# Reordering the seven-product scheme of a SwiGLU up-projection, with twice the accumulating banks

## The reference

```python
def _swiglu(x, w13, w2):
    h = x @ w13                       # (512 x 1024) @ (1024 x 5632), D_FF = 2816
    g, u = jnp.split(h, 2, axis=-1)
    return (jax.nn.silu(g) * u) @ w2
...
x = _layer_norm(ALPHA * x + _swiglu(x, ffn_w13[i], ffn_w2[i]), ln2_g[i], ln2_b[i])
```

## Time and profile before

| | |
|---|---|
| time, median of 3 runs | 2188.87 us (2188.75 to 2191.24) |
| the profiled execution | 2189.42 us, its span 2187.2 us |
| PE busy | 2153.1 us (98% of the span), 13192 matmuls |
| DVE busy | 1515.6 us (69%) |
| ACT busy | 887.5 us (41%) |
| POOL busy | 538.5 us (25%) |
| PE clock granted | full in all 40 slices |
| DMA | 204.33 MB, mean 93 GB/s |

### The profile page before, as it was taken

The page is one execution under the profiler, slowest core; times in us unless marked ns, Lnnn a source line. Parts: engine busy times, 40 slices in busy tenths (PEclk is TensorE's granted clock), DMA queues, the critical chain, the costliest instruction groups (busy, mean ns, idle before and its releaser), DMA issues.

```text
span 2187.2 us, 34709 instructions
## 1 busy us (share of the span) xinstructions
PE 2153.1 (98%) x13192; PEld 1891.8 (86%) x13192; DVE 1515.6 (69%) x2037; ACT 887.5 (41%) x1554; POOL 538.5 (25%) x370
## 2 busy tenths in 40 slices
PE   9999999999999999999999999999999999999998
PEld 7777899998888988999888899988887778999887
DVE  3787688963479977898534789943538867889434
ACT  3455444442233423444322444432325554444322
POOL 0000255620030003565200356500000003565000
PEclk9999999999999999999999999999999999999999
DMA  6211323333333022334431333342232113333421
GB/s 212 68 58 48 104 80 109 105 116 106 106 96 97 1 76 78 88 107 115 156 96 53 102 87 97 101 131 96 77 116 68 52 61 100 87 97 99 133 96 58
DMA packets 256744, 204.33 MB, mean 93 GB/s; under 512 B 6256, under 2 KB 235760, under 8 KB 256608
## 3 DMA queue, kind: packets, MB, share of 16 engines
q1 hardware_dynamic: 252976, 189.42, 29.0%
q0 software_dynamic: 3632, 13.02, 1.9%
HBM read 200.32 MB, written 2.10 MB: 93 GB/s over the span
## 4 chain that ended last, share of the span: by engine, by line
PE 91%; DVE 5%; issue 2%; ACT 1%; DMA 1%; SPq 0%; POOL 0%; DVEq 0%; POOLq 0%; ACTq 0%
PE ps L1485 18%; PE ps L1487 18%; PE ps L1486 18%; PE ps L1564 10%; PE ps L1565 9%; PE ps L1566 9%; DVE hid L1263 3%; PE ps L1779 2%; PE ps L1802 1%; PE ps L1610 1%; PE ps L1791 1%; PE ps L1782 1%; PE ps L1930 0%; PE ps L2025 0%; DVE x_nat L1026 0%
## 5 line engine op out<-in xcount | busy, mean ns | idle before, releaser
L967 DVE TENSOR_TENSOR w_lo<-raw,w_hi 128x1024 fp32r<-128x1024 f32 x212 | 278.5, 1322 | 343.2 <-ACT w_hi L586 342.4
L586 ACT ACTIVATE w_hi<-raw 128x1024 fp32r<-128x1024 f32 x212 | 220.5, 1055 | 423.9 <-PE ps L1487 372.0
L1395 DVE TENSOR_TENSOR w_lo<-raw,w_hi 128x512 fp32r<-128x512 f32 (+1 forms) x256 | 297.0, 1170 | 43.9 <-ACT w_hi L652 43.7
L1485 PE MATMUL ps<-w_hi,a_hi 128*128 128x512 f32 x832 | 325.9, 392 | 0.3 <-DVE w_lo L967 0.2
L1487 PE MATMUL ps<-w_hi,a_lo 128*128 128x512 f32 x832 | 323.9, 389 | 0.0
L1486 PE MATMUL ps<-w_lo,a_hi 128*128 128x512 f32 x832 | 323.8, 389 | 0.0
L1564 PE MATMUL ps<-t_hi,w_hi 128*128 128x256 f32 x1024 | 293.5, 287 | 4.9 <-DVE over_lo L1404 0.9
L1485 PE MATMUL ps<-xT_hi,w_hi 128*128 128x512 f32 (+1 forms) x760 | 292.6, 385 | 4.9 <-issue 3.7
L1565 PE MATMUL ps<-t_lo,w_hi 128*128 128x256 f32 x1024 | 289.6, 283 | 0.0
L1566 PE MATMUL ps<-t_hi,w_lo 128*128 128x256 f32 x1024 | 289.5, 283 | 0.0
L1487 PE MATMUL ps<-xT_hi,w_lo 128*128 128x512 f32 (+1 forms) x760 | 285.6, 376 | 0.0
(11 more groups left out here) (170 smaller groups left out, 4151.2 us busy)
## 6 DMA issues: line engine op xcount, KB each, us to landing
raw<-in_w SPq DMA_DIRECT2D x264, 512.0 KB, 4.0
raw<-in_wqkv SPq DMA_DIRECT2D x48, 512.0 KB, 3.9
raw<-in_pw SPq DMA_DIRECT2D x24, 512.0 KB, 4.1
raw<-in_wo SPq DMA_DIRECT2D x16, 512.0 KB, 3.7
ln_gb<-in_g POOLq DMA_DIRECT2D x8, 512.0 KB, 4.5
ln_gb<-in_b POOLq DMA_DIRECT2D x8, 512.0 KB, 5.8
x_nat<-in_x SPq DMA_DIRECT2D x4, 512.0 KB, 6.1
out<-x_nat SPq DMA_DIRECT2D x3, 512.0 KB, 2.6
```

What stands on the lines that cost most here:

```text
L586: nc.scalar.activation(weight_hi(u), raw[:, r, :], ACT.Copy).then_inc(w_hi_done, 1)
L967: nc.vector.tensor_tensor(weight_lo(u), raw[:, r, :], weight_hi(u).bitcast(f32), ALU.subtract).then_inc(w_lo_done, 1)
L1395: nc.vector.tensor_tensor(to, src, hi.bitcast(f32), ALU.subtract).then_inc(form_lo[g], 1)
L1485: nc.tensor.matmul(dst, lhs[0], rhs[0], start=start, stop=False, skip_group_check=check)
```

## The change

All of it lies in the seven-product stage and at its end; the products, their matmuls and the forms stay the same in number and size.

- PE's order in block p becomes A11(p), A22(p-1), S2(p), A12(p), S4(p-1), S3(p), S1(p).
- The banks: A11 and A12 use one of the banks of the whole units; S2, S3 and A22 alternate between two banks by the block's parity, and so do S1 and S4. S2 and S1 wait for the reader of two blocks before.
- S4's form has two places, by parity.
- The kept sums lie in buffers that attention uses (`mix_gb`, `o_nat`) instead of the weight ring's free quarter; u2 has two places.
- DVE's order: c22(p-1), low S4(p), low S1(p), c21(p-1), low A22(p), u2(p), gating(p-2), c12(p-1), low A1(p+1), u3(p), low S23(p+1). ACT's: high S4(p), S1(p), copy of A11(p), high A22(p), `first_tokens(p)`, high A1(p+1), `last_tokens(p-1)`, high S23(p+1).
- The loads of a block also wait for the low part of A22, now the last form made.
- At the end of the stage the splits of chunks 20 and 21 and the last sums have another order, the gating of block 14 among them; before a pooling layer POOL's loads into `mix_gb` wait for the gating of block 15.

```diff
@@ -132,9 +132,9 @@
     order = []
     for p in range(SEVENS):
         if p == 0:
-            order += [(p, f) for f in ("A11", "S2", "A12", "S1", "S3")]
+            order += [(p, f) for f in ("A11", "S2", "A12", "S3", "S1")]
         else:
-            order += [(p, "A11"), (p - 1, "A22"), (p - 1, "S4"), (p, "A12"), (p, "S2"), (p, "S1"), (p, "S3")]
+            order += [(p, "A11"), (p - 1, "A22"), (p, "S2"), (p, "A12"), (p - 1, "S4"), (p, "S3"), (p, "S1")]
     return order + [(SEVENS - 1, "A22"), (SEVENS - 1, "S4")]
 
 
@@ -142,7 +142,7 @@
 FORMS = len(FORM_NUMBER)
 G_A1, G_S1, G_S23, G_A22, G_S4 = range(5)
 FORM_GROUP = {"A11": G_A1, "A12": G_A1, "S1": G_S1, "S2": G_S23, "S3": G_S23, "A22": G_A22, "S4": G_S4}
-FORM_PLACE = {"A11": (0, 0), "A12": (0, 1), "S2": (1, 0), "S3": (1, 1), "A22": (2, 0), "S4": (2, 1), "S1": (3, 0)}
+FORM_PLACE = {"A11": (0, 0), "A12": (0, 1), "S2": (1, 0), "S3": (1, 1), "A22": (2, 0), "S1": (3, 0)}
 T3, T1, T2, T4 = range(4)
 
 
@@ -210,11 +210,8 @@
     xT_lo = sb("xT_lo", [P, KD, SEQ], f32r)
     hid = sb("hid", [P, FC * SEQ])
     raw = sb("raw", [P, RING, UNIT])
-    shared3 = -(-nc.sbuf_base // 32) * 32
     w_hi = sb("w_hi", [P, RING, UNIT], f32r)
     w_lo = sb("w_lo", [P, RING, UNIT], f32r)
-    over_hi = nc.alloc_sbuf_tensor_at("over_hi", [P, RING, UNIT], f32, offset=shared3)
-    over_lo = nc.alloc_sbuf_tensor_at("over_lo", [P, RING, UNIT], f32, offset=shared3 + RING * UNIT * 4)
     shared1 = -(-nc.sbuf_base // 32) * 32
     a_hi = sb("a_hi", [P, RING, SEQ], f32r)
     a_lo = sb("a_lo", [P, RING, SEQ], f32r)
@@ -361,18 +358,19 @@
 
         return ring_number(unit0[i, "up"] + 2 * SEVEN_TO + q) % RING
 
-    def form(tiles, i, f):
-
-        q, h = FORM_PLACE[f]
+    def form(tiles, i, p, f):
+
+        q, h = (2 + p % 2, 1) if f == "S4" else FORM_PLACE[f]
         return tiles[:, seven_slot(i, q), h * BANK:(h + 1) * BANK]
 
-    def sums_kept(i):
-
-        return [w[:, seven_slot(i, 3), BANK:2 * BANK].rearrange("p (h n) -> p h n", h=2) for w in (over_hi, over_lo)]
-
-    def seven_bank(i):
-
-        return (up_bank(i, "up") + 4) % 8
+    firsts = mix_gb[:, 0, 0:SEQ].rearrange("p (h n) -> p h n", h=2)
+    u2 = tuple(o_nat[:, 2 * h:2 * h + 2, :].rearrange("p t n -> p (t n)") for h in range(2))
+    u3 = mix_gb[:, 0, SEQ + HALF:2 * SEQ]
+
+    def seven_bank(i, p, f):
+
+        other = (up_bank(i, "up") + 4) % 8
+        return {"A11": up_bank(i, "up") + 1, "A12": up_bank(i, "up") + 1, "S1": other + 2 + p % 2, "S4": other + 2 + p % 2}.get(f, other + p % 2)
 
     def used(i, p, f):
@@ -437,6 +435,7 @@
                     if SEVEN_FROM <= c - 2 < SEVEN_TO:
                         p = SEVENS * i + c - 2 - SEVEN_FROM
                         sp.wait_ge(form_lo[G_S4], p + 1)
+                        sp.wait_ge(form_lo[G_A22], p + 1)
                         sp.wait_ge(form_lo[G_S1], p + 1)
                         sp.dma_start(raw[:, u % RING, :].rearrange("p (k n) -> p k n", n=P), src).then_inc(raw_loaded[u % RING], 16)
                     else:
@@ -533,6 +532,7 @@
                         nc.gpsimd.tensor_tensor(top[:, BANK:2 * BANK], top[:, BANK:2 * BANK], s23[:, 0, :], ALU.subtract).then_inc(form_sum, 1)
                 if to_pooling(n + 1):
                     j = (i + 1) // 3
+                    pool.wait_ge(gated, gated_before(i, "up") + SEVEN_TO)
                     pool.dma_start(mix_gb[:, 0, :], pool_s[j:j + 1, :].to_broadcast([P, D])).then_inc(mix_loaded, 16)
                     pool.dma_start(mix_gb[:, 1, :], pool_b[j:j + 1, :].to_broadcast([P, D])).then_inc(mix_loaded, 16)
                     pool.wait_ge(form_used, FORMS * (i + 1))
...
-                if p:
+                    free, src, to = "S4", top[:, BANK:2 * BANK], form(w_hi, i, p, "S4")
+                if g == G_S4 and p:
+                    if p > 1:
+                        act.wait_ge(form_used, used(i, p - 2, free))
+                elif p:
                     act.wait_ge(form_used, used(i, p - 1, free))
...
-                nc.scalar.activation(sums_kept(i)[0][:, p % 2, :], ps[:, seven_bank(i), 0:HALF], ACT.Copy).then_inc(kept, 1)
+                nc.scalar.activation(firsts[:, p % 2, :], ps[:, seven_bank(i, p, "A11"), 0:HALF], ACT.Copy).then_inc(kept, 1)
 
             def first_tokens(p):
 
                 c = SEVEN_FROM + p
                 act.wait_ge(form_used, used(i, p, "A12"))
                 act.wait_ge(gated, g0 + c - 1)
-                nc.scalar.activation(gate[:, c % 2, 0:HALF], ps[:, seven_bank(i), 0:HALF], func).then_inc(head_done, 1)
+                nc.scalar.activation(gate[:, c % 2, 0:HALF], ps[:, seven_bank(i, p, "A12"), 0:HALF], func).then_inc(head_done, 1)
@@ -688,27 +691,30 @@
                 form_high(0, G_A22)
                 form_high(0, G_S4)
                 form_high(0, G_S1)
-                keep_first(0)
-                first_tokens(0)
-                for p in range(1, SEVENS):
-                    form_high(p, G_A1)
-                    form_high(p, G_S1)
-                    form_high(p, G_S23)
+                for p in range(SEVENS):
+                    if p:
+                        form_high(p, G_S4)
+                        form_high(p, G_S1)
                     keep_first(p)
-                    form_high(p, G_A22)
-                    form_high(p, G_S4)
-                    last_tokens(p - 1)
+                    if p:
+                        form_high(p, G_A22)
                     first_tokens(p)
+                    if p < SEVENS - 1:
+                        form_high(p + 1, G_A1)
+                    if p:
+                        last_tokens(p - 1)
+                    if p < SEVENS - 1:
+                        form_high(p + 1, G_S23)
                 after = u0 + 2 * SEVEN_TO
                 act.wait_ge(form_used, used(i, SEVENS - 1, "A12"))
                 split_w(after)
                 act.wait_ge(form_used, used(i, SEVENS - 1, "S3"))
                 split_w(after + 1)
+                act.wait_ge(form_used, used(i, SEVENS - 1, "A22"))
+                split_w(after + 2)
                 act.wait_ge(form_used, used(i, SEVENS - 1, "S4"))
-                split_w(after + 2)
+                split_w(after + 3)
                 last_tokens(SEVENS - 1)
-                act.wait_ge(gated, g0 + SEVEN_TO)
-                split_w(after + 3)
                 activated(n - 2)
                 for c in range(2):
                     act.wait_ge(gated, g0 + c + 1)
...
 
-            X, Y, Z = seven_bank(i), seven_bank(i) + 1, seven_bank(i) + 2
-            firsts, (u2, u3) = sums_kept(i)[0], (sums_kept(i)[1][:, h, :] for h in range(2))
+            def bank_of(p, f):
+
+                return ps[:, seven_bank(i, p, f), 0:HALF]
 
             def make_u2(p):
 
                 dve.wait_ge(kept, SEVENS * i + p + 1)
                 dve.wait_ge(form_used, used(i, p, "S2"))
-                nc.vector.tensor_tensor(u2, firsts[:, p % 2, :], ps[:, Y, 0:HALF], ALU.add).then_inc(u2_done, 1)
-
-            def make_u3_c22(p):
+                nc.vector.tensor_tensor(u2[p % 2][:, :], firsts[:, p % 2, :], bank_of(p, "S2"), ALU.add).then_inc(u2_done, 1)
+
+            def make_u3(p):
+
+                dve.wait_ge(form_used, used(i, p, "S3"))
+                nc.vector.tensor_tensor(u3, firsts[:, p % 2, :], bank_of(p, "S3"), ALU.add).then_inc(u3_done, 1)
+
+            def make_c22(p):
 
                 c = SEVEN_FROM + p
-                dve.wait_ge(form_used, used(i, p, "S3"))
-                nc.vector.tensor_tensor(u3, firsts[:, p % 2, :], ps[:, Y, 0:HALF], ALU.add).then_inc(u3_done, 1)
+                dve.wait_ge(form_used, used(i, p, "S1"))
                 dve.wait_ge(u3_done, SEVENS * i + p + 1)
-                nc.vector.tensor_tensor(hid[:, c * SEQ + HALF:(c + 1) * SEQ], u3, ps[:, Z, 0:HALF], ALU.add).then_inc(c22_done, 1)
+                nc.vector.tensor_tensor(hid[:, c * SEQ + HALF:(c + 1) * SEQ], u3, bank_of(p, "S1"), ALU.add).then_inc(c22_done, 1)
 
             def make_c21(p):
 
                 c = SEVEN_FROM + p
                 dve.wait_ge(form_used, used(i, p, "A22"))
-                nc.vector.tensor_tensor(hid[:, c * SEQ:c * SEQ + HALF], firsts[:, p % 2, :], ps[:, Y, 0:HALF], ALU.add).then_inc(c21_done, 1)
+                nc.vector.tensor_tensor(hid[:, c * SEQ:c * SEQ + HALF], firsts[:, p % 2, :], bank_of(p, "A22"), ALU.add).then_inc(c21_done, 1)
 
             def make_c12(p):
 
                 c = SEVEN_FROM + p
                 dve.wait_ge(form_used, used(i, p, "S4"))
                 dve.wait_ge(u2_done, SEVENS * i + p + 1)
-                nc.vector.tensor_tensor(gate[:, c % 2, HALF:SEQ], u2, ps[:, Z, 0:HALF], ALU.add).then_inc(c12_done, 1)
+                nc.vector.tensor_tensor(gate[:, c % 2, HALF:SEQ], u2[p % 2][:, :], bank_of(p, "S4"), ALU.add).then_inc(c12_done, 1)
 
             def gating_seven(p):
 
@@ -1449,27 +1460,34 @@
             form_low(0, G_S4)
             gating(3)
             form_low(0, G_S1)
```

(71 more changed lines are left out.)

## The result

The changed kernel takes 2239.67 us (median of 4 runs, 2237.93 to 2241.53), the one before 2189.20 (median of 4). The ratio is 1.0229, with a 95% interval of 1.0211 to 1.0247: 50.5 us slower, where 2237 and so +48 was forecast. The profiled execution has a span of 2235.8 us.

A forecast was written before the change was run, and what follows sets the result against it. PE bounded the kernel before, and DVE would set the loop's pace after. 4 x (12.8 loop + 3.0 end) - 15.5 of old stalls = +47.7 us, so 2237 us; forecast's own range 2222 to 2252, 8 in 10 2195 to 2254.

The forecast's parts named there:

- 15.5 us: PE's stalls over the four stages of the kernel before, 0.7%, claimed as all that the loop could give.
- the one stall of 0.24 in front of S3: PE's wait for u2 in the kernel before, read as 3.9 us a layer over 15 blocks.
- The distances on PE: In the loop, two products instead of one before S3 and A22; by this alone all 15.5 us go.
- The block of 11.15: DVE's list for one loop block laid out at 11.15 us against PE's 10.08, so PE waits 1.07 a block.
- the round trip: In each block DVE's gating, ACT's silu and high A1, then DVE's low A1: 1.40 us on ACT's side.
- 12.8: Forecast PE wait in the loop, us a layer: 11.8 for blocks 4 to 14 plus 1.0 for blocks 1 to 3.
- the three turns: In each block POOL's sums against DVE's low S4, S1 and A22 at the port: 1.71 us each, 5.13 together.
- The end: At the stage's end chunk 20 waits for block 14's gating behind two splits: PE stands 3.0 us a layer.
- The full hold: Rival: port lock held without early handover, block 12.05 us, time 2280; 0.05, shared with anything above 2254.
- POOL in front of the pooling layer: POOL's sums before the pooling layer move behind block 15's gating: taken as 0, bounds 2.9 us either way.

The follow-up runs named there:

- experiment 4: Kernel before, POOL's four sums half as wide (half of the columns left out) except in the first block: 2175.60 us, ratio 0.9927.
- experiment 9: Kernel before, its banks and product order kept, with u2(p) moved ahead of the gating of block p-1 in DVE's list: 2175.65 us, ratio 0.9930.
- experiment 1: Changed kernel with the gating of block p-2 first in DVE's block instead of behind u2(p): 2200.98 us, ratio 1.0052.
- experiment 3: Changed kernel with POOL's four sums half as wide (half of the columns left out) except in the first block: 2190.49 us, ratio 1.0000.
- experiment 7: Kernel before with the gating of block 14 moved behind the first split, u3, c22 of block 15 and the second split: 2210.84 us, ratio 1.0089.
- experiment 2: Changed kernel with the gating of block 14 ahead of the two splits at the stage's end: 2226.51 us, ratio 1.0158.
- experiment 5: Changed kernel with the gating of block p-2 first in DVE's block and that of block 14 ahead of the splits: 2190.19 us, ratio 1.0001.
- experiment 6: Changed kernel with both gatings moved earlier, and u2(p) ahead of c21(p-1) and low A22(p) in DVE's list: 2176.11 us, ratio 0.9936.
- experiment 10: Changed kernel with both gatings and u2 early, run once more on the same chip as the kernel before with u2 early: 2176.03 us, ratio 0.9934.

## Why the prediction was right

**What bounds, and what there was to win.** 15.5 us was the right ceiling: experiments 4 and 9 reach 0.2 and 0.3 us of stalls and gain 14 to 15 us.

**Where the stalls of before stood.** Here the prediction read too little of the trace. It took the one stall of 0.24 in front of S3 for all of them, "a quarter of a microsecond for each of 15 blocks". By the starts of all products only 5.8 of the 15.5 us stand in front of S3, and 9.5 in front of A22, which waits for u3. The same block as in the earlier trace rows, PE and DVE:

```profile
384.48 0.28 PE L1566 MATMUL ps<-xT_hi,w_lo 128*128 128x256 f32 x1
384.87 0.36 PE L1564 MATMUL ps<-t_hi,w_hi 128*128 128x256 f32 x1
```

```profile
384.31 0.41 DVE L1410 TENSOR_TENSOR over_lo<-over_hi,ps 128x256 f32<-128x256 f32 x1
```

The stall is 384.87 - 384.48 - 0.12 = 0.27, and u3 comes right behind the low S1 that POOL holds up (1.74 at 382.65). The sum 15.5 and the forecast do not depend on this, but the question why u2 is late was little more than a third of the question.

**The distances on PE.** They did what they say: no stall in front of A22, S4, S2, S1 or A12 in any block of the changed kernel. But they were worth nothing of their own: with DVE's list in order, experiment 9 has no stalls at the old distances either.

**The block of 11.15.** It measured 11.16, with its parts: the low parts at 1.4 to 1.8, low S23 at 2.20, 1.12 of idle in front of low A1 (1.1 was named), 0.67 and 0.28 in front of S3 and A11 (0.7 and 0.4 were named). Experiments 1 and 3 take away one cause each: without the round trip 33 of the loops' 47.9 us go, and with short turns all of them. So the block was far over PE's 10.08 only by both together. 12.0 us a layer were measured against 12.8: that the three turns always fall together was a little too strict. In two to four of the blocks 5 to 14 of each layer one of the two stalls is missing. In block 10 of the first layer, one of them, the load landed late: POOL's L523 started only at 412.38, after 2.00 us of waiting for it, and DVE's first two low parts passed in 1.28 together instead of 3.15.

**The end.** 2.97 against 3.0 a layer, by the chain named (2.85 of wait and 0.12 of slow start).

**What was missing.** The half clock behind the end's stall, 4.8 us. It makes up for the 3.2 us by which the loops were forecast too dear, so that the sum of 63.2 came within 1.4 us of the measured 64.6 is partly luck. Without the half clock the time would have been some 5 us less, still well inside the range.

**The full hold** would have given a block of 12.05. The rows of the changed kernel again show the handover early: POOL's sum of 390.41 ended at 391.98, and DVE's low part behind it, 0.68 long, at 392.53 (389.38 + 3.15), so it began at 391.85, 0.13 before. The lock that the Trainium skill describes (SBUF — State Buffer, "Who interferes with whom") holds here but for this 0.13.

**POOL in front of the pooling layer** was taken as 0. The whole difference of the spans is in the four stages but for half a microsecond, so nothing larger stands there.

## What to carry to other kernels

When PE stands in front of a product, ask what its supplier has queued in front of each sum that PE waits for, before giving PE more banks or distance: one line moved in the old kernel won as much as the repaired new scheme. List the stalls of a whole stage by product first; one of them may not be typical. In an order written by hand, follow each wait around the engines: here DVE gated a block just before it needed a part from ACT, and ACT could make that part only after a step that waited for this gating, so two lists that had overlapped became one round trip. Where two engines take turns at the port, a move also changes who comes first, so look at both engines' rows after it. And check that the last block's order still delivers what the stage behind it waits for.

## What the runs showed of the hardware

- A pause of PE can cost more than its length. Behind the stall of 3.0 to 3.3 us the granted clock fell to 1.2 GHz in 9 of 16 cases (the changed kernel, experiments 1, 3 and 7), which cost 1.6 us, and up to 2.8 in the kernel before with the late end. Before the fall PE had been at full clock and then stood for those 3 us. Behind 0.6 us (16 cases: experiments 2, 5, 6 and 10) and 1.5 us (4 cases) it never fell, nor behind the loops' 0.7. Why it fell in 9 of the 16 and not in the other 7 stays open.
- After a short stall the first matmul's record is 0.36 long instead of 0.28, and the second starts 0.19 after it instead of 0.12: a stall costs 0.07 more than its wait.
- Of a DVE instruction with two SBUF inputs and a POOL sum the one that begins first is not held up, even by little: before, POOL's began 0.11 before DVE's (382.54 and 382.65), took 1.30 and DVE's 1.74; in experiment 9 DVE's was first, and POOL's took 1.68.
- Making two engines take turns at the port costs nothing where both have slack. In experiment 9 POOL is busy for 99 us a stage, the most of all, and PE has no stalls.
